# Value rows of the experts: summed by VectorE on the residual row instead of by TensorE in PSUM

## The chip, the cores and the metric

One core of one Trainium2 chip runs the whole step. The metric is the device time of one execution in microseconds (us). The kernel before took 2659.16 us (median of three runs, 2646.86 to 2667.52). The engines are called as in the profile: PE (TensorE matmul), PEld (its weight loads), DVE (VectorE), ACT (ScalarE), POOL (GpSimd), SP (SyncE). POOL issues the gathers, SP the loads of the weights.

## The reference, cut to what matters

One layer runs over 512 prompt rows and 32 sample rows of width 1024, in float32. It has two kinds of attention, output projections, and then a layer of experts (PEER): for each row, 8 heads pick 16 experts each out of 16384, so 128 experts a row. Of an expert, one row of `u` makes a score and one row of `v` is added, weighted:

```python
ue = jnp.take(u, eidx, axis=0)
act = jax.nn.gelu(jnp.einsum("nhkd,nd->nhk", ue, xb), approximate=False)
ve = jnp.take(v, eidx, axis=0)
return jnp.einsum("nhk,nhkd->nd", (g * act.astype(jnp.float32)).astype(ve.dtype), ve)
...
x = x + _peer(_rmsnorm(x, norm2_g), ...)
y = rmsnorm(x) * final_g
```

`xb` is the normed row, `g` the softmax over the 16 scores of a head. Every row needs its own 128 rows of `u` and `v`, so they are gathered from memory, 8 KB for a pair.

## The kernel before, in words

**Tiles.** The 544 rows are five tiles: four of 128 prompt rows (a row to a partition), and the 32 sample rows. A tile has a *front* (attention, projections, the choice of its experts) and its *slots*: slot j gathers the j-th expert of each of the 128 rows, a block of 128 x 2048 floats, 1 MB. A tile of prompt rows has 128 slots; the sample tile packs its 32 x 128 experts onto 128 partitions and has 32. In all there are 544 slots.

**A slot.** POOL waits until the ring slot is free and issues the gather (`gather`, L600) into one of six ring buffers (`RING = 6`). DVE takes the dot product of the `u` half with `xb` (`dot`, L1552, which the trace shows as a long instruction and a short read of the accumulator). ACT takes the gelu (L898). The `v` half is then added in one of two ways, as the table `ADDERS` says:
- PE: DVE writes a diagonal matrix gelu x weight (`weigh`, L1563; nine buffers, `DIAGS`), and PE multiplies it with the `v` half into the PSUM accumulator `acc` (`add_v`, L1217). A float32 matmul stands in the trace as several records.
- DVE: it makes the coefficient in a column (L1570) and adds coefficient x `v` onto `vsum` (`add_v`, L1577).

Four slots are a *block*, two a *half*. In the first 11 blocks of the kernel three of four slots go to DVE; in blocks 19 to 29 of each prompt tile all go to PE; else the last of four goes to DVE. PE opens `acc` with the residual row `x2` (`seed`, L1207), and adds `vsum` at the end (`close`, L1228). `finish` norms `acc` and stores the result.

**The order.** All engines walk one list, `PLAN`, each in its own program order. While the slots of tile t run, the front of tile t+1 is spread between its 64 halves (`spread`), in pieces: attention first (DVE takes a maximum of scores that PE has just made, L1411; ACT exponentiates; PE turns and multiplies), then the projections, whose weights SP loads in chunks of 1 MB through three buffers (`wbuf`; DVE works on their results at L1421 and L1432, ACT at L874), then the scores and the top-k search on DVE (L1438, L1443, L1449). On DVE a half is two dots and then two `weigh` or `add_v`, and the piece of the front comes behind it. PE runs the adds of a half after the pieces of that half. The sample tile's slots run last, in a loop, with no front beside them.

A ring slot is free for the next gather when its dot is taken and the engine that adds its value row is done with it.

## Time and profile before

| | |
|---|---|
| time, median of 3 runs | 2659.16 us (2646.86 to 2667.52) |
| span of the profiled execution, first to last instruction | 2671.0 us |
| PE busy | 2152.5 us, 81% of the span |
| DVE busy | 1434.8 us, 54% |
| ACT busy | 524.8 us, 20% |
| POOL busy | 671.1 us, 25% |
| data moved by DMA | 765.82 MB, of which the gathers' queue moved 570.46 MB |

The profiled execution is one more execution, not among the three; its span is 11.8 us above their median and 3.5 us above the highest. Busy time is time in which an engine has an instruction running; a busy PE is not a PE at its peak, since its matmuls overlap. The fronts and the slots load the engines differently, so the shares over the whole span are means over stages. The slots run from about 496 us to the end.

### The profile page before, as it was taken

To read this page: it belongs to the slowest core of one execution; us is meant where nothing else is said; L and a number is where in the kernel's file an instruction comes from. 1 tells how busy PE (TensorE), PEld (TensorE's weight loads), DVE (VectorE), ACT (ScalarE), POOL (GpSimd) and SP (SyncE) were. 2 spreads that over 40 slices of the span, in tenths; PEclk is the share of its full clock that TensorE was granted. 3 is DMA by queue.
4 is the path that set the end of the run, shared out by engine and by line. 5 is a ranking of instruction groups with operands and counts; after the bars stand their busy time and mean duration, and the time that the engine had idled before them with its cause. 6 is when DMAs were issued, how large, how long until landed. Compare 5 with 4: busy or idle time off the path is not lost. (4 is left out here: it accounts for less than half of the span.)

```text
span 2671.0 us, 23686 instructions
## 1 busy us (share of the span) xinstructions
PE 2152.5 (81%) x7804; PEld 1230.3 (46%) x7804; DVE 1434.8 (54%) x3480; ACT 524.8 (20%) x1354; POOL 671.1 (25%) x694
## 2 busy tenths in 40 slices
PE   7989889987698876897887778888765898987766
PEld 6845566455346632444562234456322344664211
DVE  0111105654554397666448865654795566337956
ACT  2321111110341101441110133301111332010111
POOL 0000000233222133233223422322333223223433
PEclk9988999999678987888998887999987787778788
DMA  9832455798769987678999866799989567888887
GB/s 275 272 91 86 136 185 173 290 361 316 266 231 333 331 322 298 257 272 325 367 376 334 346 243 247 299 378 334 396 308 387 221 248 285 304 310 310 313 329 314
DMA packets 271239, 765.82 MB, mean 287 GB/s; under 512 B 22736, under 2 KB 191744, under 8 KB 201488
## 3 DMA queue, kind: packets, MB, share of 16 engines
q0 software_dynamic: 78336, 570.46, 55.6%
q1 hardware_dynamic: 156848, 155.52, 18.6%
q10 hardware_dynamic: 35936, 38.35, 4.3%
q8 instruction: 62, 1.02, 0.2%
q14 instruction: 57, 0.47, 0.0%
HBM read 745.56 MB, written 18.30 MB: 286 GB/s over the span
## 5 line engine op out<-in xcount | busy, mean ns | idle before, releaser
L1217 PE MATMUL acc<-ring,diag 128*128 128x512 f32 (+1 forms) x1720 | 950.3, 705 | 272.2 <-DVE diag L1563 264.7
L600 POOL DMA_INDIRECT ring<-in_uv,stage x544 | 614.0, 1129 | 1471.1 <-PE acc L1217 877.0
L1552 DVE CUSTOM_DVE_ANT_0 ring<-ring,xb 128x1024 f32<-128x1024 f32 x544 | 651.5, 1221 | 209.1 <-DMA ring<-in_uv,stage 199.7
L1217 PEld LDWEIGHTS acc<-ring,diag 128*128 128x128 f32 (+1 forms) x1720 | 362.2, 222 | 783.4 <-issue 425.9
L898 ACT ACTIVATE gel<-dots 128x1 f32<-128x1 f32 x544 | 105.6, 201 | 1059.0 <-DVE dots L1552 1040.8
L1563 DVE TENSOR_SCALAR diag<-ident,gel,gw 128x128 f32<-128x128 f32 x406 | 141.8, 357 | 213.0 <-ACT gel L898 200.7
L1001 PE MATMUL pz<-F,wbuf 128*128 128x416 f32 (+1 forms) x656 | 244.8, 533 | 3.6 <-issue 1.4
L1001 PEld LDWEIGHTS pz<-F,wbuf 128*128 128x128 f32 (+1 forms) x656 | 127.1, 196 | 114.7 <-issue 114.7
L618 POOL COPY stage<-idx 128x4 int32<-128x4 int32 x130 | 50.9, 392 | 505.6 <-DVE gw L1511 486.6
L1411 DVE TENSOR_REDUCE nmax<-ps 128x1 f32<-128x128 f32 (+4 forms) x72 | 35.6, 495 | 236.9 <-PE ps L1058 81.5
L1577 DVE SCALAR_TENSOR_TENSOR vsum<-ring,coefd,vsum 128x1024 f32<-128x1024 f32 x109 | 140.3, 1287 | 4.0
L1183 PE MATMUL ps<-F,wbuf 128*128 128x128 f32 (+1 forms) x1024 | 132.3, 291 | 10.2 <-DMA wbuf<-in_peer_wq 5.9
L1183 PEld LDWEIGHTS ps<-F,wbuf 128*128 128x128 f32 x1024 | 130.1, 208 | 22.0 <-issue 13.5
L898 ACT ACT_TABLE_LOAD x65 | 83.4, 1283 | 26.2 <-issue 22.5
L1001 PE MATMUL pz<-wbuf,F 128*128 128x256 f32 (+1 forms) x384 | 85.7, 383 | 0.0
L1001 PE MATMUL pz<-ring,wbuf 128*128 128x128 f32 (+1 forms) x656 | 79.5, 280 | 6.7 <-PE pz L1001 2.8
L1001 PEld LDWEIGHTS pz<-ring,wbuf 128*128 128x128 f32 (+1 forms) x656 | 75.1, 190 | 13.9 <-issue 11.2
L1411 DVE TENSOR_REDUCE nmax<-pz 128x1 f32<-128x256 f32 (+3 forms) x48 | 28.6, 596 | 96.9 <-PE pz L1050 46.5
L1138 PEld LDWEIGHTS ps<-F,wbuf 128*128 128x128 f32 x512 | 69.1, 218 | 17.8 <-issue 6.5
L1001 PEld LDWEIGHTS pz<-wbuf,F 128*128 128x128 f32 (+1 forms) x384 | 65.8, 172 | 21.8 <-issue 5.4
L1138 PE MATMUL ps<-F,wbuf 128*128 128x128 f32 (+1 forms) x512 | 69.7, 300 | 6.9 <-ACT F L829 3.4
L1076 PE MATMUL pt<-ident,F 128*128 128x128 f32 (+2 forms) x224 | 34.3, 271 | 47.8 <-DVE F L1396 47.6
(259 smaller groups left out, 1954.4 us busy)
## 6 DMA issues: line engine op xcount, KB each, us to landing
wbuf<-in_w_in SPq DMA_DIRECT2D x52, 1024.0 KB
wbuf<-in_peer_wq SPq DMA_DIRECT2D x40, 1024.0 KB
wbuf<-in_w_pa SPq DMA_DIRECT2D x20, 1024.0 KB
wbuf<-in_w_o SPq DMA_DIRECT2D x20, 1024.0 KB
wbuf<-in_w_pb SPq DMA_DIRECT2D x20, 512.0 KB
ring<-in_uv,stage POOLq DMA_INDIRECT x544
zT<-F ACTq DMA_DIRECT2D x28, 208.0 KB, 2.9
qT<-zT ACTq DMA_DIRECT2D x4, 768.0 KB, 6.8
```

The lines of the kernel that those rows point to most:

```text
L600: pool.indirect_dma_start(out=ring[:, slot, :], out_offset=None, in_=d["uv"], in_offset=bass.IndirectOffsetOnAxis(ap=stage[:, a, k:k + 1], ...
L618: nc.gpsimd.tensor_copy(stage[:, a, :], idx[:, t % 2, BLOCK * b:BLOCK * b + BLOCK]).then_inc(staged[a], 1)
L898: nc.scalar.activation(gel[:, slot:slot + 1], dots[:, slot:slot + 1], ACT.Gelu).then_inc(gelued, 1)
L1001: last = nc.tensor.matmul(out, left, right, start=(k == 0), stop=(k == KT - 1))
L1076: last = nc.tensor.transpose(pt[0:w, j * nq:(j + 1) * nq], p[0:nq, j * P:j * P + w], ident[0:nq, 0:nq])
L1138: last = nc.tensor.matmul(ps[f % 2][:, 0:nq], wa[:, k, j * P:(j + 1) * P], fa(t).oaT[:, k, 0:nq], start=(k == 0), stop=(k == 7))
L1183: last = nc.tensor.matmul(ps[f % 2][:, 0:nq], w[:, k, j * P:(j + 1) * P], fa(t).xbT[:, k, 0:nq], start=(k == 0), stop=(k == 7))
L1217: last = nc.tensor.matmul(acc[0:nq, c * 512:(c + 1) * 512], diag[:, parity, 0:nq], ring[:, slot, D + c * 512:D + (c + 1) * 512], start=Fal ...
L1411: nc.vector.tensor_reduce(nmax[0:nq, n:n + 1], score_bank(t, n)[0:nq, 0:nk], AX.X, ALU.max, negate=True).then_inc(maxed, 1)
L1552: nc.vector.tensor_tensor_reduce(out=u, in0=u, in1=xb[:, t % 2, :], scale=1.0, scalar=0.0, op0=ALU.mult, op1=ALU.add, accum_out=dots[:, sl ...
L1563: nc.vector.tensor_scalar(diag[:, parity, 0:nq], pick[:, 0:nq], gel[:, slot:slot + 1], g, ALU.mult, ALU.mult).then_inc(coef_set, 1)
L1577: last = nc.vector.scalar_tensor_tensor(vsum[:, :], v, c, vsum[:, :], ALU.mult, ALU.add)
```

## The change

- `ADDERS`, `vsum`, `diag`, `coefd` and the accumulator `acc` are gone. DVE adds every value row (`add_v`): coefficient x `v` onto `xsum`, a pair of buffers of which a tile uses one, and in which the front has put the residual row. PE takes no part in the slots, but for two matmuls at the end of the kernel that fold the sample tile's four groups of partitions (`fold`).
- ACT makes the coefficient: behind each gelu it multiplies by the expert's weight into a column `cf` (`weigh`).
- A gather waits for DVE's add alone. DVE's add waits for ACT's coefficient and for the add before it.
- The attention of tile t+1 no longer waits for PE's `seed`: `xsum` has two buffers, and its operand `foxq` lies in the one that tile t-1 used, so it waits for that tile's result.
- The sample tile's slots are written out, not looped.

```diff
-DIAGS = 9
-EARLY = 11
-LATE = (19, 30)
...
-    return plan + [("experts_loop", TILES - 1, 0), ("finish", TILES - 1, 0)]
+    plan += [("experts", TILES - 1, b) for b in range(SLOTS // 4 // HALF)]
+    return plan + [("finish", TILES - 1, 0)]
...
-    counts, out = {"tensor": 0, "vector": 0}, []
-    for s in range(SLOTS * (TILES - 1) + SLOTS // 4):
-        who_early = "vector" if s < BLOCK * EARLY and s % BLOCK else None
-        late = s < SLOTS * (TILES - 1) and LATE[0] <= s % SLOTS // BLOCK < LATE[1]
-        who = "vector" if s % BLOCK == BLOCK - 1 and not late else "tensor"
-        who = who_early or who
-        counts[who] += 1
-        out.append((who, counts[who]))
...
-        vsum = sb("vsum", [P, D])
-        coefd = sb("coefd", [P, STAGES])
+        xsum = sb("xsum", [P, 2, D])
+        cf = sb("cf", [P, RING])
...
+        def y_sum(t):
+
+            return ps_all[0:DEC, :] if t == TILES - 1 else xsum[:, t % 2, :]
+
+        def foxq(t):
+
+            return xsum[0:16, t % 2, :].rearrange("p (h q) -> p h q", h=HEADS)
...
                     if s >= RING:
-                        who, count = ADDERS[s - RING]
-                        waits = [(dotted, s - RING + 1), (adders[who], count)]
+                        waits = [(v_added, s - RING + 1)]
                     gather(k, a, s % RING, waits)
...
-            def gelu(slot, count):
-                act.wait_ge(dotted, count)
+            def gelu(s):
+
+                slot = s % RING
+                act.wait_ge(dotted, s + 1)
                 nc.scalar.activation(gel[:, slot:slot + 1], dots[:, slot:slot + 1], ACT.Gelu).then_inc(gelued, 1)
 
+            def weigh(t, s, j):
+
+                slot = s % RING
+                act.wait_ge(gelued, s + 1)
+                nc.scalar.activation(cf[:, slot:slot + 1], gel[:, slot:slot + 1], ACT.Copy, scale=gw[:, t % 2, j:j + 1]
+                                     ).then_inc(weighed, 1)
+
             def experts(t, b, h):
-                s0 = SLOTS * t + BLOCK * b + HALF * h
-                for s in range(s0, s0 + HALF):
-                    gelu(s % RING, s + 1)
-
...
+                j0 = BLOCK * b + HALF * h
+                if j0 == 0:
+                    act.wait_ge(route_ready, t + 1)
+                    if t == TILES - 1:
+                        act.wait_ge(packed, 16 * 9)
+                for j in range(j0, j0 + HALF):
+                    gelu(SLOTS * t + j)
+                    weigh(t, SLOTS * t + j, j)
...
             def finish(t):
                 nq = rows_of(t)
-                act.wait_ge(summed, t + 1)
-                act.wait_ge(dotted, SLOTS * t + slots_of(t))
-                rms_sum(xb[0:nq, t % 2, :], acc[0:nq, :], nq, 8)
+                act.wait_ge(v_added, SLOTS * t + slots_of(t))
+                if t == TILES - 1:
+                    act.wait_ge(summed, 1)
+                rms_sum(xb[0:nq, t % 2, :], y_sum(t), nq, 8)
                 rms_root_(nq, 8, 9)
                 act.wait_ge(y_ready, t + 1)
...
-            def add_v(t, slot, parity, count):
-
-                nq = rows_of(t)
-                pe.wait_ge(coef_set, count)
-                for c in range(2):
-                    last = nc.tensor.matmul(acc[0:nq, c * 512:(c + 1) * 512], diag[:, parity, 0:nq],
-                                            ring[:, slot, D + c * 512:D + (c + 1) * 512],
-                                            start=False, stop=False, skip_group_check=True)
-                last.then_inc(v_added, 1)
-
...
-            def close(t):
-
-                nq = rows_of(t)
-                pick = ident if t < TILES - 1 else sel32
-                pe.wait_ge(v_added_dve, v_adds("vector", SLOTS * t + slots_of(t)))
-                for c in range(2):
-                    last = nc.tensor.matmul(acc[0:nq, c * 512:(c + 1) * 512], pick[:, 0:nq],
-                                            vsum[:, c * 512:(c + 1) * 512], start=False, stop=True,
-                                            skip_group_check=True)
...
+            def fold(t):
...
+                pe.wait_ge(v_added, SLOTS * t + slots_of(t))
                 for c in range(2):
...
+                    last = nc.tensor.matmul(ps[c][0:nq, :], sel32[:, 0:nq], xsum[:, t % 2, c * 512:(c + 1) * 512],
+                                            start=True, stop=True)
                 last.then_inc(summed, 1)
...
-            held = None
             for what, t, p in PLAN:
-                if what in ("experts", "experts_loop") and held:
-                    experts(*held)
-                    held = None
-                if what == "experts":
-                    if p == 0:
-                        seed(t)
-                    held = (t, p // 2, p % 2)
-                elif what == "experts_loop":
-                    seed(t)
-                    experts_loop(t)
-                elif what in pe_stages:
+                if what in pe_stages:
                     pe_stages[what](t, p)
+            fold(TILES - 1)
...
-                if t:
-                    dve.wait_ge(seeded, t)
+                if t >= 2:
+                    dve.wait_ge(y_ready, t - 1)
+                if t == TILES - 1:
+                    nc.vector.memset(xsum[DEC:2 * DEC, t % 2, :], 0.0).then_inc(rest_cleared, 1)
+                    nc.vector.memset(xsum[2 * DEC:P, t % 2, :], 0.0).then_inc(rest_cleared, 1)
...
-            def weigh(t, slot, parity, g, gelus, adds):
-
-                nq = rows_of(t)
-                if adds is not None:
-                    dve.wait_ge(v_added, adds)
-                dve.wait_ge(gelued, gelus)
-                pick = ident if t < TILES - 1 else sel32
-                nc.vector.tensor_scalar(diag[:, parity, 0:nq], pick[:, 0:nq], gel[:, slot:slot + 1], g,
-                                        ALU.mult, ALU.mult).then_inc(coef_set, 1)
...
-            def add_v(slot, turn, g, gelus, coefs, adds):
-
-                dve.wait_ge(gelued, gelus)
-                c = coefd[:, turn:turn + 1]
-                nc.vector.tensor_scalar(c, gel[:, slot:slot + 1], g, None, ALU.mult).then_inc(coefd_set, 1)
-                dve.wait_ge(coefd_set, coefs)
-                v = ring[:, slot, D:2 * D]
-                if adds is None:
-                    last = nc.vector.tensor_scalar(vsum[:, :], v, c, None, ALU.mult)
-                else:
-                    dve.wait_ge(v_added_dve, adds)
-                    last = nc.vector.scalar_tensor_tensor(vsum[:, :], v, c, vsum[:, :], ALU.mult, ALU.add)
-                last.then_inc(v_added_dve, 1)
...
+            def add_v(t, s):
+
+                slot = s % RING
+                dve.wait_ge(weighed, s + 1)
+                dve.wait_ge(v_added, s)
+                total = xsum[:, t % 2, :]
+                nc.vector.scalar_tensor_tensor(total, ring[:, slot, D:2 * D], cf[:, slot:slot + 1], total,
+                                               ALU.mult, ALU.add).then_inc(v_added, 1)
...
             def experts(t, b, h):
-                if b == 0 and h == 0:
+                j0 = BLOCK * b + HALF * h
+                if j0 == 0:
...
+                        dve.wait_ge(rest_cleared, 2)
+                half = range(SLOTS * t + j0, SLOTS * t + j0 + HALF)
+                for s in half:
+                    dot(t, s)
+                for s in half:
+                    add_v(t, s)
...
-                dve.wait_ge(summed, t + 1)
-                nc.vector.scalar_tensor_tensor(xb[0:nq, t % 2, :], acc[0:nq, :], sstat[0:nq, 8:9], gfrow[0:nq, :],
+                nc.vector.scalar_tensor_tensor(xb[0:nq, t % 2, :], y_sum(t), sstat[0:nq, 8:9], gfrow[0:nq, :],
                                                ALU.mult, ALU.mult).then_inc(y_ready, 1)
```

What moves. On DVE, in the top-k search of the third tile, which lies beside the second tile's slots (blocks 19 and 20 of that tile; `MAX` is the search, the two `ISA` rows are a dot and the read of its sum), before:

```order
L1563 TENSOR_SCALAR diag<-ident,gel,gw 128x128 x2
L1438 MAX F<-F 128x8 x16
L1552 ISA ring,dots<-ring,xb 128x1024
L1552 ISA dots 128x1
L1552 ISA ring,dots<-ring,xb 128x1024
L1552 ISA dots 128x1
L1563 TENSOR_SCALAR diag<-ident,gel,gw 128x128 x2
```

and of the change:

```order
L1335 MAX F<-F 128x8 x16
L1450 ISA ring,dots<-ring,xb 128x1024
L1450 ISA dots 128x1
L1450 ISA ring,dots<-ring,xb 128x1024
L1450 ISA dots 128x1
L1460 SCALAR_TENSOR_TENSOR xsum<-ring,cf,xsum 128x1024 x2
```

Two diagonals of 128 columns have become two adds of 1024 columns; the number of dots and the search stand as they were.

On DVE, in the attention of the third tile beside the second tile's slots (`nmax` is the maximum that waits for PE's scores), before:

```order
L1411 TENSOR_REDUCE nmax<-pz 128x1 x2
L1552 ISA ring,dots<-ring,xb 128x1024
L1552 ISA dots 128x1
L1552 ISA ring,dots<-ring,xb 128x1024
L1552 ISA dots 128x1
L1563 TENSOR_SCALAR diag<-ident,gel,gw 128x128
L1570 TENSOR_SCALAR coefd<-gel,gw 128x1
L1577 SCALAR_TENSOR_TENSOR vsum<-ring,coefd,vsum 128x1024
```

and of the change:

```order
L1308 TENSOR_REDUCE nmax<-pz 128x1 x2
L1450 ISA ring,dots<-ring,xb 128x1024
L1450 ISA dots 128x1
L1450 ISA ring,dots<-ring,xb 128x1024
L1450 ISA dots 128x1
L1460 SCALAR_TENSOR_TENSOR xsum<-ring,cf,xsum 128x1024 x2
```

A half that had one diagonal, one coefficient and one add has two adds; the maxima keep their place ahead of the next half.

On PE, from the last projection of the second tile's front to the attention of the third tile's (`kaT` x `qT`), before:

```order
L1183 MATMUL ps<-F,wbuf 128x128 x48
L1217 MATMUL acc<-ring,diag 128x512 x4
L1183 MATMUL ps<-F,wbuf 128x128 x32
L1195 MATMUL ps<-wbuf,F 128x128 x16
L1217 MATMUL acc<-ring,diag 128x512 x68
L1228 MATMUL acc<-vsum,ident 128x512 x2
L1207 MATMUL acc<-x2,ident 128x512 x2
L1217 MATMUL acc<-ring,diag 128x512 x4
L1036 MATMUL ps<-kaT,qT 128x384
L1050 MATMUL ps<-bias,ident 128x256
```

and of the change:

```order
L1121 MATMUL pt<-ident,xb 128x128 x4
L1121 MATMUL po<-ident,xb 128x128 x4
L1134 MATMUL ps<-F,wbuf 128x128 x128
L1146 MATMUL ps<-wbuf,F 128x128 x16
L987 MATMUL ps<-kaT,qT 128x384
L1001 MATMUL ps<-bias,ident 128x256
```

The matmuls of the projection follow each other with none of the slots' between them, and the next tile's attention follows them at once in PE's program.

## Rows read from the trace of the kernel before

**Rows 1.** The page: busy us of each engine; ACT's gelus (busy, mean ns, idle before).

```profile
PE 2152.5 (81%) x7804; PEld 1230.3 (46%) x7804; DVE 1434.8 (54%) x3480; ACT 524.8 (20%) x1354; POOL 671.1 (25%) x694
...
L898 ACT ACTIVATE gel<-dots 128x1 f32<-128x1 f32 x544 | 105.6, 201 | 1059.0 <-DVE dots L1552 1040.8
```

**Rows 2.** Stages (windows): length, busy PE, PEld, DVE, ACT, POOL; granted clock; DMA share, GB/s.

```profile
495.90:641.00 145.10, 131.26 (x477) 83.98 (x476) 92.62 (x150) 16.62 (x68) 51.66 (x48) 0.96 0.94 357
698.70:805.30 106.60, 94.16 (x273) 48.00 (x272) 62.83 (x149) 53.20 (x109) 24.72 (x30) 0.80 0.63 228
805.30:943.70 138.40, 122.20 (x655) 90.82 (x654) 55.09 (x134) 20.11 (x57) 26.01 (x29) 0.93 0.94 330
943.70:1031.00 87.30, 56.22 (x93) 21.88 (x92) 84.65 (x266) 7.74 (x27) 28.74 (x30) 0.80 0.76 288
...
1055.50:1209.50 154.00, 130.46 (x361) 63.13 (x361) 98.46 (x208) 65.95 (x132) 42.49 (x49) 0.83 0.74 279
1209.50:1388.30 178.80, 145.00 (x702) 101.99 (x703) 89.61 (x192) 23.40 (x74) 48.34 (x50) 0.90 0.97 351
1388.30:1512.50 124.20, 89.21 (x160) 35.98 (x159) 108.75 (x315) 10.98 (x43) 52.75 (x50) 0.84 0.89 337
...
2219.30:2411.30 192.00, 168.57 (x680) 112.46 (x679) 83.58 (x181) 20.71 (x76) 47.62 (x47) 0.73 0.85 300
2411.30:2540.50 129.20, 97.80 (x202) 41.00 (x201) 111.50 (x332) 13.11 (x47) 52.06 (x51) 0.84 0.84 318
...
2575.60:2671.00 95.40, 56.88 (x101) 11.69 (x100) 59.07 (x111) 9.08 (x36) 39.00 (x34) 0.80 0.85 344
```

**Rows 3.** Who waited for whom, whole span: us in total, times, longest us.

```profile
POOL ring L600 <- PE acc L1217: 877.0, 154, 22.0
DVE diag L1563 <- ACT gel L898: 201.7, 52, 13.6
DVE ring L1552 <- DMA ring<-in_uv,stage: 199.7, 139, 6.2
```

**Rows 4.** Timeline of DVE in attention: start, us, instruction, idle before it and its releaser.

```profile
1128.12 0.56 DVE L1411 TENSOR_REDUCE nmax<-pz 128x1 f32<-128x384 f32 x1 [1.84 <-PE pz L1050]
1129.59 0.56 DVE L1411 TENSOR_REDUCE nmax<-pz 128x1 f32<-128x384 f32 x1 [0.91 <-PE pz L1050]
1130.06 1.22 DVE L1552 CUSTOM_DVE_ANT_0 ring<-ring,xb 128x1024 f32<-128x1024 f32 x1
...
1132.97 1.28 DVE L1577 SCALAR_TENSOR_TENSOR vsum<-ring,coefd,vsum 128x1024 f32<-128x1024 f32 x1
1134.18 1.22 DVE L1552 CUSTOM_DVE_ANT_0 ring<-ring,xb 128x1024 f32<-128x1024 f32 x1
...
1137.15 0.16 DVE L1391 RECIPROCAL rinv<-rsum 128x2 f32<-128x2 f32 x1
```

**Rows 5.** Timeline of DVE in the top-k search.

```profile
1447.96 1.22 DVE L1552 CUSTOM_DVE_ANT_0 ring<-ring,xb 128x1024 f32<-128x1024 f32 x1
...
1450.26 0.77 DVE L1563 TENSOR_SCALAR diag<-ident,gel,gw 128x128 f32<-128x128 f32 x2
1450.94 1.22 DVE L1552 CUSTOM_DVE_ANT_0 ring<-ring,xb 128x1024 f32<-128x1024 f32 x1
```

**Rows 6.** Groups by line, 1055.5 to 1209.5 us: busy, mean ns, idle before, releasers.

```profile
L1411 DVE TENSOR_REDUCE nmax<-ps 128x1 f32<-128x384 f32 x12 | 6.7, 558 | 29.2 <-PE ps L1050 17.9 <-PE ps L1058 10.7 <-issue 0.5
L1411 DVE TENSOR_REDUCE nmax<-pz 128x1 f32<-128x384 f32 x12 | 6.7, 558 | 21.4 <-PE pz L1050 14.2 <-PE pz L1058 7.2
```

**Rows 7.** Granted clock beside two such pieces (windows, columns as in rows 2).

```profile
1126.00:1130.00 4.00, 3.93 (x17) 2.30 (x18) 1.25 (x4) 2.44 (x4) 1.19 (x2) 1.00 0.76 252
1614.00:1619.00 5.00, 5.00 (x12) 2.67 (x12) 1.33 (x3) 1.71 (x3) 0.00 (x0) 0.50 0.79 315
```

**Rows 8.** Timeline of DVE in the second of them.

```profile
1615.21 0.69 DVE L1411 TENSOR_REDUCE nmax<-pz 128x1 f32<-128x512 f32 x1 [2.66 <-PE pz L1050]
1618.36 0.69 DVE L1411 TENSOR_REDUCE nmax<-pz 128x1 f32<-128x512 f32 x1 [2.46 <-PE pz L1050]
```

132 lines of the change are left out of this document (12 added, 120 removed).

## The prediction, made before the result

> **What bounds the kernel now.** The page says that PE is the busiest engine, 81% against DVE's 54% [rows 1]. That invites the thought that taking work off PE must help. The means hide stages with different limits, so I read the stages next, then who waited for whom, then DVE's own timeline.
>
> Cut by what the next tile's front does, the slots of one tile fall into three long stages [rows 2]. POOL's count tells how many slots a stage holds: a block of four slots is four gathers and one copy, so x50 is ten blocks and x30 six.
> - Attention (1055.5 to 1209.5 us): ten blocks in 154.0 us. DVE is busy 98.5 us and DMA only 0.74. What fills DVE's gaps are the maxima, which wait 50.6 us for PE's scores [rows 6]. The timeline [rows 4] shows how: DVE waits 1.84 and 0.91 us in a piece, and then works through the slots without a pause: 1130.06 to 1137.15 is one block, and the next piece begins at once. DVE is never short of a gathered row there. DVE and its round trip to PE set the pace.
> - Projections (1209.5 to 1388.3 us): DMA share 0.97 at 351 GB/s. The weights share the DMA engines with the gathers, and DMA sets the pace. The same stage beside the first and the fourth tile's slots has DMA 0.94 and 0.85, with PE busy 122.2 of 138.4 us and 168.6 of 192.0 us: there PE has a part in it.
> - Top-k search (1388.3 to 1512.5 us): DVE is busy 108.8 of 124.2 us, and beside the first tile's slots 84.7 of 87.3 us. DVE is the bound.
>
> POOL waits 877.0 us for PE's adds [rows 3]. That number is large and mostly harmless: a gather that goes out later costs only where DVE then finds its row missing, and that wait is 199.7 us in the whole kernel.
>
> **The change, part by part.**
>
> *DVE per block.* Two dots take 2.30 us (1447.96 to 1450.26 in rows 5). An add of 1024 columns takes 1.28 us, and what follows it starts after 1.21 us (1132.97 to 1134.18 in rows 4). Of the two adds of a half, the second waits for the first one's end, so I put 2.52 us for the pair. A half is 4.82 us, a block 9.64 us. Before, a block with one add by DVE took 7.09 us [rows 4], and one with none 2 x 2.98 = 5.96 us [rows 5]. So a block gains 2.55 us in attention and 3.68 us in the top-k search.
>
> *Attention.* The four prompt tiles have 6 + 10 + 10 + 10 = 36 such blocks (the first tile has fewer, since projections precede them). 36 x 2.55 = **+92 us**. Nothing hides it, as DVE works through its slots without a pause.
>
> *Top-k search.* Again 36 blocks: 36 x 3.68 = 132 us. DVE is idle 2.6, 15.5 and 17.7 us in three of the four stages [rows 2], and I take 15 for the fourth, together some 50 us. Those waits are for gathered rows, at the start of the stage, while the extra work is spread over it. I let 27 us of them take it up: **+105 us** (ends 82 and 132).
>
> *Waits for PE in attention.* This is where PE's relief can show. Twelve pieces wait 50.6 us, 4.2 us each, so some 202 us in four fronts. With PE at 2.4 GHz (granted clock 1.00 [rows 7]) a piece waits 2.75 us [rows 4]; at 1.2 GHz (granted clock 0.50 [rows 7]) 2.66 + 2.46 = 5.12 us [rows 8]. Without the slots' matmuls ahead of them the scores are never late, but PE also has less to do, and the granted clock can fall more often. All 48 pieces fast would be 132 us, -70; all slow 246 us, +44. I take **0**, between the two, and keep both ends.
> The Trainium skill (TensorE: Matmul & The Clock Gate, "What's actually happening") says that the throttled state is the default and activity releases it, so it speaks against taking matmuls away. By it alone the end of +44 would hold. The trace shows both levels in this phase, so I don't go all the way.
>
> *Projections.* The first and the fourth tile's slots moved 330 GB/s x 138.4 us and 300 GB/s x 192.0 us; at the 351 GB/s of the second tile's they would take 130 and 164 us: -8 and -28. In the two stages that are already at 0.97, DVE has 89 us idle for an extra 25.5 us each, and I put +3 each for the part that lands behind a wait in DVE's program order. Together **-30 us**. Ends: -46, if the 0.97 goes to 1 as well (two times 5 us) and nothing is paid; +15, if the two stages pay all of their 25.5 us.
>
> *The start of the first tile's slots* (495.9 to 641.0 us): three of four adds are DVE's already, DMA share 0.94. **-8 us** (ends -9 and 0).
>
> *The sample tile* (2575.6 to 2671.0 us): eight blocks x 9.64 = 77 us of DVE in 95.4 us. DMA share is 0.85, and the gathers need no longer go round by PE. **-5 us** (ends -14 and 0).
>
> *ACT.* One more instruction a slot, which I put at the gelu's 0.20 us [rows 1]: 109 us for an engine that is 20% busy. The first coefficient is made while DVE takes the second dot (1.15 us). Where ACT comes late from the exponentials of a piece, the add waits 0.2 us more; behind the add stand the next dots, the next piece of the front, and by it PE. 48 such halves give 10 us at most; **+6 us** (ends 0 and 25, if all 272 halves pay 0.1 us).
>
> *What else moves.* POOL waits for DVE's add alone; its order is the same. `seed` and `close` go, ten pairs of matmuls, which the 0 above includes. The wait of the attention for the last tile's result is over when `finish` is, and that stands ahead of it on DVE already: nothing. SP's weights wait for PE as before.
>
> *Sum:* 92 + 105 + 0 - 30 - 8 - 5 + 6 = +160 us. The profiled execution's span was 2671.0 us, so 2831 us, and as it lies 11.8 us above the median of the runs, **2819 us** for the median, 6% above 2659.
>
> **The rivals.**
> - *Cold PE.* All pieces wait as in rows 8 (+44) and the projections, whose matmuls then run at 1.2 GHz more often, give nothing back (+30): 2893 us. For it: the granted clock of every stage is below 1, down to 0.73, so that parts of each ran at the lower level, with PE busy for most of the time [rows 2]. Against: in the projections PE works in long bursts, and there the granted clock is 0.93 and 0.90 beside the first two tiles' slots, if only 0.73 beside the fourth's [rows 2]. This is the skill's rule above, as a mechanism of this kernel.
> - *Nothing absorbed.* DVE's waits in program order are not filled: the top-k search pays 132, not 105, and the projections +15, not -30: +72, 2891 us. For it: DVE cannot work on slots while its next instruction waits for a projection. Against: in those stages it waits for gathered rows too, and that wait takes extra work for free.
> - *Fast PE.* All pieces at 2.75 us (-70), the projections at -46, the top-k search at 82: 2659 + 160 - 70 - 16 - 23 = 2710 us.
> - *PE was the bound after all (faster).* The extra DVE work is some 92 + 132 + 92 in the projections' 36 blocks + 20 in the sample tile, 336 us. If DVE's waits for gelus (201.7 us), which are delayed by PE in ACT's program order, and for gathered rows (199.7 us) both go [rows 3], that is 401 us back, and 2659 + 336 - 401 = 2594 us. It decides from 336 us of relief on. For it: 81% against 54% and POOL's 877 us. Against: neither wait is long in the attention and the top-k stages, where two thirds of the extra work lies, and DMA at 0.97 does not let the waits of the projections go.
> - *A draw.* The relief is about the extra work, 2660 us: it needs both ends of the projections and of the waits for PE, and an idle DVE in the top-k stages that I don't see.
>
> **How the numbers follow.** Forecast 0.55, own range 2765 to 2875 us. Cold PE 0.12, nothing absorbed 0.08, fast PE 0.10, faster 0.07, a draw 0.08. The first four are slower by more than 1% (about what a measurement can tell here): 0.85; within 1% 0.08; faster 0.07. The range from 2715 to 2910 us leaves out the faster case, the draw and the outer part of fast PE below, and a few per cent above.
>
> **What would show it.** In the profile after: DVE busy about 1434.8 + 544 - 109 adds more at 1.28 us (557) less 430 diagonals at 0.385 (0.77 for two [rows 5]; 166), so about 1825 us, and near 97% in the top-k stage, which takes 150 us instead of 124; the attention stage 180 us instead of 154; a piece's waits between 2.75 and 5.1 us; the projections of the second tile within 6 us of 178.8; POOL waiting for DVE's adds where it waited for PE. The forecast is wrong if the attention stage stays near 154 us or if DVE waits long for gelus or rows in the top-k stage.

## The result, and the profile after

The changed kernel takes **2951.4 us** (median of 4 runs, 2948.0 to 2958.2) where the kernel before takes 2662.0 us (median of 4): a ratio of 1.112 (95% interval 1.108 to 1.117). I had forecast slower, 2819 us with a range from 2715 to 2910 us. The sign was right, the size was not: the profiled spans differ by 2946.8 - 2671.0 = 275.8 us, and I had 160.

The page of the kernel after: busy time, granted clock in 40 slices, and the groups of the experts (busy, mean ns | idle before, releaser).

```profile
PE 1412.8 (48%) x6048; PEld 990.1 (34%) x6048; DVE 1811.2 (61%) x3368; ACT 678.4 (23%) x1898; POOL 829.2 (28%) x694
...
PEclk9988999985568555556765555577655555555555
...
L576 POOL DMA_INDIRECT ring<-in_uv,stage x544 | 771.6, 1418 | 1586.5 <-DVE xsum L1460 1456.6
...
L1460 DVE SCALAR_TENSOR_TENSOR xsum<-ring,cf,xsum 128x1024 f32<-128x1024 f32 x544 | 697.9, 1283 | 256.8 <-ACT cf L855 228.4
L1450 DVE CUSTOM_DVE_ANT_0 ring<-ring,xb 128x1024 f32<-128x1024 f32 x544 | 645.3, 1220 | 25.8 <-DMA ring<-in_uv,stage 23.9
...
L855 ACT ACTIVATE cf<-gel,gw 128x1 f32<-128x1 f32 x544 | 160.2, 295 | 17.7
```

PE fell from 81% [rows 1] to 48%, DVE rose to 61%, and no engine is now busy for two thirds of the span. DVE's busy time, 1811.2 us, is where the forecast had it (1825). The second line is the news. From the tenth slice on, the granted clock is mostly 5, which is PE's lower level, 1.2 GHz, throughout a slice. A gathered row is hardly ever late any more: 23.9 us, where DVE waited 199.7 [rows 3].

Who waited for whom, columns as in [rows 3]:

```profile
POOL ring L576 <- DVE xsum L1460: 1456.6, 222, 23.2
DVE xsum L1460 <- ACT cf L855: 228.4, 89, 20.5
```

POOL now waits for DVE as it waited for PE. DVE's wait for ACT has not gone with PE's work: 201.7 us for the gelu became 228.4 us for the coefficient.

The stages after, in windows with the columns of [rows 2]. They are cut at the same slots as before: the first 40 slots, then attention, projections and top-k search beside the first tile's slots, the same and the plain rest beside the second's, projections and top-k search beside the fourth's, and the sample tile.

```profile
498.10:633.30 135.20, 116.90 (x440) 79.42 (x439) 96.76 (x120) 29.93 (x109) 61.04 (x51) 0.94 0.98 384
691.40:831.40 140.00, 79.81 (x200) 45.82 (x200) 79.08 (x144) 58.77 (x133) 29.28 (x30) 0.50 0.47 172
831.40:974.20 142.80, 87.90 (x564) 80.31 (x564) 76.60 (x134) 27.07 (x81) 35.48 (x30) 0.80 0.92 324
974.20:1083.40 109.20, 0.00 (x0) 0.00 (x0) 107.08 (x267) 14.81 (x51) 33.03 (x29) 0.50 0.61 222
1102.90:1316.70 213.80, 104.64 (x241) 54.91 (x241) 125.19 (x200) 76.08 (x172) 57.57 (x51) 0.51 0.55 210
1316.70:1500.90 184.20, 100.05 (x579) 91.49 (x579) 115.34 (x184) 34.95 (x114) 63.34 (x52) 0.73 0.96 347
1500.90:1649.10 148.20, 0.00 (x0) 0.00 (x0) 145.26 (x314) 22.77 (x83) 63.76 (x49) 0.50 0.72 276
1649.10:1668.60 19.50, 0.00 (x0) 0.00 (x0) 19.08 (x25) 3.98 (x16) 14.19 (x11) 0.50 0.99 377
2482.50:2667.80 185.30, 126.17 (x582) 112.48 (x581) 110.36 (x171) 32.66 (x117) 62.59 (x49) 0.55 0.86 311
2667.80:2821.20 153.40, 3.55 (x20) 2.73 (x18) 148.18 (x331) 24.31 (x86) 68.38 (x50) 0.51 0.70 267
2853.60:2946.80 93.20, 3.62 (x4) 0.54 (x4) 80.03 (x103) 19.79 (x69) 35.55 (x34) 0.50 0.84 350
```

Summed over the four prompt tiles, from both traces ("start" is the first 48 slots):

| stage | before | after | change | forecast |
|---|---|---|---|---|
| before the first slot | 495.9 | 498.1 | +2 | 0 |
| start of the first tile's slots | 202.9 | 193.3 | -10 | -8 |
| attention | 620.0 | 813.6 | **+194** | +92 and 0 for waits |
| projections | 684.7 | 698.6 | **+14** | -30 |
| top-k search | 462.3 | 559.1 | +97 | +105 |
| plain rest of a tile | 109.9 | 90.9 | -19 | none |
| sample tile | 95.3 | 93.2 | -2 | -5 |

(ACT's +6 stood in no one stage.) So the top-k search, both ends of the program and DVE's own work were foreseen. The miss lies in the attention, about 100 us, and in the projections, 44 us.

In the second tile's attention stage the window says how the loss splits. It is 213.8 - 154.0 = 59.8 us longer. DVE is busy 125.19 - 98.46 = 26.7 us longer, against the 10 x 2.55 that I had. Most of the rest is in two groups, the maxima that wait for PE's scores:

```profile
L1308 DVE TENSOR_REDUCE nmax<-ps 128x1 f32<-128x384 f32 x12 | 6.7, 557 | 46.6 <-PE ps L1001 31.6 <-PE ps L1009 14.9
L1308 DVE TENSOR_REDUCE nmax<-pz 128x1 f32<-128x384 f32 x12 | 6.7, 556 | 34.3 <-PE pz L1001 22.8 <-PE pz L1009 11.5
```

80.9 us where it was 50.6 [rows 6], +30.3 us. Over the 48 pieces the sum in the traces went from 230.6 to 320.4 us, +90. (The forecast had started from 202, the second tile's mean times 48.) DVE's timeline beside such a piece (columns as in [rows 4]):

```profile
1206.19 0.56 DVE L1308 TENSOR_REDUCE nmax<-pz 128x1 f32<-128x384 f32 x1 [3.46 <-PE pz L1001]
1208.92 0.56 DVE L1308 TENSOR_REDUCE nmax<-pz 128x1 f32<-128x384 f32 x1 [2.17 <-PE pz L1001]
1209.40 1.21 DVE L1450 CUSTOM_DVE_ANT_0 ring<-ring,xb 128x1024 f32<-128x1024 f32 x1
...
1212.06 2.67 DVE L1460 SCALAR_TENSOR_TENSOR xsum<-ring,cf,xsum 128x1024 f32<-128x1024 f32 x2 [0.30 <-ACT cf L855]
1214.65 1.22 DVE L1450 CUSTOM_DVE_ANT_0 ring<-ring,xb 128x1024 f32<-128x1024 f32 x1
...
1216.94 2.67 DVE L1460 SCALAR_TENSOR_TENSOR xsum<-ring,cf,xsum 128x1024 f32<-128x1024 f32 x2
1219.53 0.16 DVE L1288 RECIPROCAL rinv<-rsum 128x2 f32<-128x2 f32 x1
```

The piece waits 3.46 + 2.17 = 5.63 us; the same piece of before waited 2.75 [rows 4]. The block behind it runs from 1209.40 to 1219.53, 10.13 us with a wait of 0.30 for ACT, so 9.83 of work against the 9.64 that I had summed. The granted clock is 0.50 in this piece and in each of the 48; before, it was 1.00 throughout in 22 of them.

The first piece of a tile is a case of its own. Its queries `qT` are loaded by ACT's queue, and the load now lands late:

```profile
1111.32 0.38 ACTq L791 DMA_DIRECT2D qT<-zT  x1
...
1127.14 1.61 PE L987 MATMUL ps<-kaT,qT 64*128 64x384 f32 x2 [159.87 <-DMA qT<-zT]
...
1129.95 0.56 DVE L1308 TENSOR_REDUCE nmax<-ps 128x1 f32<-128x384 f32 x1 [12.57 <-PE ps L1001]
```

These rows say that DVE stands idle for 12.57 us because PE began at 1127.14, 15.8 us after the load was issued. The first pieces of the four fronts wait 60.0 us together, where it was 42.8. So of the +90 us, 17 are theirs and 73 belong to the 44 ordinary pieces (187.8 to 260.4 us).

### The profile page after: what moved, and what is told of

Same layout as the page of the kernel before. It is cut to its first block, busy times and chain, and to the rows that moved or that the text cites. A ratio compares the mean times of both kernels' runs of the same rounds, so it can differ in the third digit from the quotient of the medians.

```text
span 2946.8 us, 20298 instructions
## 1 busy us (share of the span) xinstructions
PE 1412.8 (48%) x6048; PEld 990.1 (34%) x6048; DVE 1811.2 (61%) x3368; ACT 678.4 (23%) x1898; POOL 829.2 (28%) x694
## 4 chain that ended last, share of the span: by engine, by line
PE 38%; DVE 33%; DMA 12%; issue 8%; ACT 7%; ACTq 1%; SPq 0%; DVEq 0%; POOL 0%; PEldq 0%; POOLq 0%
DVE xsum L1460 16%; PE pz L952 13%; DVE ring L1450 6%; PE ps L1134 5%; PE ps L987 3%; PE ps L1089 3%; PE pz L987 2%; ACT L849 2%; DMA wbuf<-in_peer_wq 2%; DVE F L1340 2%; DMA wbuf<-in_w_o 2%; DMA wbuf<-in_w_pa 2%; DMA qT<-zT 2%; DMA wbuf<-in_w_in 2%; PE ps L1111 2%
## 5 line engine op out<-in xcount | busy, mean ns | idle before, releaser
L576 POOL DMA_INDIRECT ring<-in_uv,stage x544 | 771.6, 1418 | 1586.5 <-DVE xsum L1460 1456.6
L1460 DVE SCALAR_TENSOR_TENSOR xsum<-ring,cf,xsum 128x1024 f32<-128x1024 f32 x544 | 697.9, 1283 | 256.8 <-ACT cf L855 228.4
L1450 DVE CUSTOM_DVE_ANT_0 ring<-ring,xb 128x1024 f32<-128x1024 f32 x544 | 645.3, 1220 | 25.8 <-DMA ring<-in_uv,stage 23.9
L987 PE MATMUL ps<-kaT,qT 64*128 64x128 f32 (+4 forms) x96 | 64.2, 766 | 622.8 <-DMA qT<-zT 401.4
L987 PEld LDWEIGHTS ps<-kaT,qT 64*128 64x128 f32 (+1 forms) x96 | 19.3, 254 | 638.3 <-issue 636.6
L1134 PE MATMUL ps<-F,wbuf 128*128 128x128 f32 (+1 forms) x1024 | 161.7, 328 | 43.1 <-DMA wbuf<-in_peer_wq 33.5
L1134 PEld LDWEIGHTS ps<-F,wbuf 128*128 128x128 f32 x1024 | 156.7, 246 | 48.7 <-DMA wbuf<-in_peer_wq 34.4
L1027 PE MATMUL pt<-ident,F 128*128 128x128 f32 (+2 forms) x224 | 52.9, 377 | 240.4 <-DVE F L1293 240.4
L855 ACT ACTIVATE cf<-gel,gw 128x1 f32<-128x1 f32 x544 | 160.2, 295 | 17.7
L1027 PEld LDWEIGHTS pt<-ident,F 128*128 128x128 f32 (+2 forms) x224 | 36.2, 221 | 253.2 <-DVE F L1293 252.0
L1089 PE MATMUL ps<-F,wbuf 128*128 128x128 f32 (+1 forms) x512 | 94.5, 365 | 55.5 <-DMA wbuf<-in_w_pa 27.1
L1089 PEld LDWEIGHTS ps<-F,wbuf 128*128 128x128 f32 x512 | 91.9, 282 | 58.8 <-DMA wbuf<-in_w_pa 28.1
```

Source lines behind the costliest of these rows:

```text
L576: pool.indirect_dma_start(out=ring[:, slot, :], out_offset=None, in_=d["uv"], in_offset=bass.IndirectOffsetOnAxis(ap=stage[:, a, k:k + 1], ...
L855: nc.scalar.activation(cf[:, slot:slot + 1], gel[:, slot:slot + 1], ACT.Copy, scale=gw[:, t % 2, j:j + 1]).then_inc(weighed, 1)
L987: nc.tensor.matmul(s[0:nq, 0:bank], q, kk[:, 0:bank], start=True, stop=False)
L1027: last = nc.tensor.transpose(pt[0:w, j * nq:(j + 1) * nq], p[0:nq, j * P:j * P + w], ident[0:nq, 0:nq])
L1089: last = nc.tensor.matmul(ps[f % 2][:, 0:nq], wa[:, k, j * P:(j + 1) * P], fa(t).oaT[:, k, 0:nq], start=(k == 0), stop=(k == 7))
L1134: last = nc.tensor.matmul(ps[f % 2][:, 0:nq], w[:, k, j * P:(j + 1) * P], fa(t).xbT[:, k, 0:nq], start=(k == 0), stop=(k == 7))
```

## The experiments

Theory 1, formed on these rows: PE, left with little to do, runs at 1.2 GHz, and each piece's scores come later to a DVE that waits for them. The rivals: DVE's longer work alone makes the loss (the adds, or the coefficients from ACT), or the order of the instructions on DVE does.

A ratio is against the kernel before, measured again beside the run (medians 2653.0 to 2664.9 us). The changed kernel was not, so differences from its 2951.4 us carry a few us of that spread. Stages are read from the profiled execution.

### e1: the changed kernel, PE kept busy through all slots

```diff
+        spare = psum("spare", 512)
...
+            def beat(t, b, h):
+                for k in range(HALF * h, HALF * h + HALF):
+                    pe.wait_ge(dotted, SLOTS * t + BLOCK * b + k + 1)
+                    for c in range(2):
+                        nc.tensor.matmul(spare[:, 0:512], ident[:, :], gfrow[:, 0:512], start=True, stop=True)
...
+                if what == "experts":
+                    if held is None:
+                        pe.wait_ge(rows_landed, 32)
+                    else:
+                        beat(*held)
+                    held = (t, p // 2, p % 2)
```

> The changed kernel, with two matmuls of 128x512 per slot given back to PE, behind the slot's dot, from constants into a spare bank: no result of theirs is used and nobody waits for them. Theory 1 (the clock): the changed kernel is slow beyond DVE's extra work because PE, left with little to do, runs at the lower clock, and DVE waits for its scores. Then the granted clock comes back to 0.8 or more, a piece of attention waits some 4.2 us where it waited 6.7, and the time falls by 48 x 2.5 = 120 us less what the new matmuls cost in PE's order: about 2850 us (2810 to 2890). Theory 2 (DVE's work and the order alone): the clock does not matter, the time stays within 15 us of 2951 or rises.

Measured: 2961.6 us, ratio 1.117 (1.109 to 1.125), mean clock 0.861. Theory 1's 2850 us missed, and the total is what theory 2 said, although the clock came back as theory 1 wanted. The stages say more (their execution took 2942.5 us, the fastest of five): attention 813.6 to 746.2 us, but the start of the first tile's slots 193.3 to 239.5 and the projections 698.6 to 714.0. The second tile's attention stage, and PE's groups from 500 to 700 us of this run:

```profile
1134.90:1332.10 197.20, 153.69 (x394) 74.19 (x393) 125.33 (x200) 76.57 (x172) 57.59 (x51) 0.78 0.60 229
```

```profile
L1167 PE MATMUL spare<-gfrow,ident 128*128 128x512 f32 x170 | 75.5, 597 | 3.1 <-DVE dots L1465 1.7
L953 PE MATMUL pz<-wbuf,F 128*128 128x256 f32 x288 | 63.1, 379 | 0.0
```

At a clock of 0.78 instead of 0.51 the stage is 16.6 us shorter with the same work on DVE. At the start PE is full with projections, and the spare matmuls take 75.5 us of its time. Two effects of opposite sign, so the next job separates them (e5).

### e2: the changed kernel, half of each value row added

```diff
-                total = xsum[:, t % 2, :]
-                nc.vector.scalar_tensor_tensor(total, ring[:, slot, D:2 * D], cf[:, slot:slot + 1], total,
+                total = xsum[:, t % 2, 0:512]
+                nc.vector.scalar_tensor_tensor(total, ring[:, slot, D:D + 512], cf[:, slot:slot + 1], total,
```

> The changed kernel, where DVE adds only 512 of the 1024 columns of every value row (the other half of the sum is left out): an add takes some 0.53 us less, 544 of them 290 us. Theory 1 and 2 alike have DVE as the bound in attention and the top-k search, 72 blocks of four slots: 153 us less at least; if the projections pay DVE's work too, all 144 us more of theirs and the rest: 2951 - 153 = 2798 us if they don't, down to 2680 us if they do. A rival by which the clock alone sets the time: less than 60 us faster.

Measured: 2804.9 us, ratio 1.056 (1.049 to 1.064). Top-k search 559.1 to 485.0 us, -74, and attention -60; projections only -5.5. The second tile's top-k stage:

```profile
1460.00:1587.50 127.50, 0.00 (x0) 0.00 (x0) 124.30 (x316) 22.77 (x83) 57.40 (x48) 0.50 0.82 312
```

DVE is busy 124.30 of 127.50 us, before the edit 145.26 of 148.20: 21.0 us less work, 20.7 us less time. Between these two the top-k stage is DVE's work and nothing else. The projections, on the other hand, hardly follow DVE. The total is near the 2798 us expected if they don't.

### e3: the kernel before, PE's matmuls of the slots on 64 columns instead of 512

```diff
-                    last = nc.tensor.matmul(acc[0:nq, c * 512:(c + 1) * 512], diag[:, parity, 0:nq],
-                                            ring[:, slot, D + c * 512:D + (c + 1) * 512],
+                    last = nc.tensor.matmul(acc[0:nq, c * 512:c * 512 + 64], diag[:, parity, 0:nq],
+                                            ring[:, slot, D + c * 512:D + c * 512 + 64],
```

> The kernel before, where PE's adds take 64 of every 512 columns (the rest of the sum is left out); DVE, ACT, POOL and the DMAs do all that they did. Theory 1: the granted clock falls to 0.65 or so, a piece's wait rises from 4.7 to 5.6 us or more (48 of them: +45 to +95 us), while waits for gelus and for free ring slots fall; the time goes up, to about 2700 us, though PE has less to do. Theory 2: less work on PE can only help: 2600 to 2660 us.

Measured: 2718.3 us, ratio 1.025 (1.017 to 1.032). Work was only taken away, and the kernel is slower by 53 us (the kernel before had 2664.9 us beside it). Its mean clock is 0.671 where before had 0.861. The second tile's attention stage and its maxima:

```profile
1056.00:1233.60 177.60, 128.83 (x361) 78.29 (x361) 98.41 (x208) 65.73 (x132) 45.72 (x47) 0.54 0.65 237
```

```profile
L1411 DVE TENSOR_REDUCE nmax<-ps 128x1 f32<-128x384 f32 x12 | 6.7, 558 | 39.0 <-PE ps L1050 22.4 <-PE ps L1058 16.6
L1411 DVE TENSOR_REDUCE nmax<-pz 128x1 f32<-128x384 f32 x12 | 6.7, 558 | 35.0 <-PE pz L1050 22.8 <-PE pz L1058 12.3
```

This is the cleanest run of all. DVE is busy 98.41 us, as before (98.46). The clock fell from 0.83 to 0.54, the maxima wait 74.0 us instead of 50.6 (+23.4), and the stage is 177.6 - 154.0 = 23.6 us longer. It holds in the kernel before, with none of the change's other edits. All four attention stages together lose 82 us, and the 48 waits grow by 84 (230.6 to 314.8), all of it in the ordinary pieces (the first ones take 43.3 us against 42.8). The projections gain 14 us, the top-k search 17 and the first slots 8. The time was expected at about 2700 us.

### e4 and e8: the changed kernel, the work of a piece parted on DVE

A piece on DVE is two things: it merges and stores what the last piece made (which frees buffers for PE and ACT), and takes the maxima of the new scores. In the change both stand behind the half's adds. e4 puts the first part between the dots and the adds, e8 ahead of the dots (`between()` above the first loop). The maxima stay behind the adds.

```diff
+            def experts(t, b, h, between=None):
...
                 for s in half:
                     dot(t, s)
+                if between:
+                    between()
                 for s in half:
                     add_v(t, s)
...
+                    if then == "front" and ATTEND <= q < NORM_O:
+                        experts(t, p // 2, p % 2, lambda: attend_a(i, q - ATTEND))
+                        attend_b(i, q - ATTEND)
...
```

> The changed kernel with DVE's program order altered: the first part of an attention piece (the merge that PE waits for, and the stores) stands between the two dots and the two adds of the half before it, the maxima stay behind the adds. If DVE's waits for PE's scores are on the path, 2.5 us of each is now covered by the adds: 48 x 2.5 = 120 us less, 2830 us. If something else sets the pace there (the gathers, ACT), the time stays within 20 us of 2951.

> The changed kernel with the first part of an attention piece ahead of the half's dots, so that dots and adds (4.8 us) cover PE's round trip, where e4 covered it by the adds alone (2825 us, DVE's waits for scores 212 us). If the exponentials that the merge needs are ready by then: 48 x 2.3 us less again, 2825 - 90 = 2735 us. If ACT is not done with them, DVE waits for ACT in place of PE: 2790 to 2830 us.

Measured: e4 2824.9 us, ratio 1.064 (1.057 to 1.072); e8 2777.0 us, ratio 1.044 (1.040 to 1.049). The clock stays low (0.656 in both). Attention falls from 813.6 to 688.6 and to 639.6 us, and the waits for scores from 320 to 212 and to 142 us; nothing else moves by more than 7 us. e4 is where it was expected (2830 us); e8 lies between its two cases (2735, or 2790 to 2830), and DVE's wait for ACT's coefficients is no longer there than in the changed kernel (216.0 us against 228.4). So a late score costs most where nothing stands between the merge and the maxima. The slower clock does its harm through that open round trip: it is a wait of the order as much as of the clock.

### e5: the changed kernel, PE kept busy beside the attention alone

As e1, with `beat` called for halves 22 to 35 of the first tile and 0 to 21 of the others:

```diff
-                        beat(*held)
+                        n = 2 * held[1] + held[2]
+                        if 22 <= n < 36 if held[0] == 0 else n < 22:
+                            beat(*held)
```

> As e1 (matmuls that nobody waits for), but only beside the pieces of attention, so that the projections of the first tile's start are left alone. In e1 the attention stages fell from 814 to 746 us in all, and that start and the projections grew by 62 us. Theory 1 (the clock slows the attention): attention 746 us again, the rest as in the changed kernel, 2951 - 67 = 2884 us (2870 to 2900). Theory 2 (what e1 gained and lost were one thing, work moved from one stage to the other): about 2950 us.

Measured: 2886.1 us, ratio 1.087 (1.081 to 1.092), 65 us below the changed kernel. The second tile's attention stage and its maxima:

```profile
1080.90:1279.00 198.10, 157.24 (x393) 76.36 (x393) 125.27 (x199) 75.96 (x171) 57.67 (x51) 0.77 0.60 225
```

```profile
L1325 DVE TENSOR_REDUCE nmax<-ps 128x1 f32<-128x384 f32 x12 | 6.7, 558 | 41.2 <-PE ps L1002 28.6 <-PE ps L1010 12.7
L1325 DVE TENSOR_REDUCE nmax<-pz 128x1 f32<-128x384 f32 x12 | 6.7, 556 | 23.8 <-PE pz L1002 15.9 <-PE pz L1010 7.9
```

Matmuls whose results nobody reads were added, DVE has the same work (125.27 us against 125.19), and the stage is 15.7 us shorter, for 15.9 us less of waiting (80.9 to 65.0). With e3 this shows theory 1 from both sides. Over all 48 pieces the waits fall from 320 to 265 us and the attention stages by 55 us. That is 55 of the 73 us of the ordinary pieces; the first pieces stay at 60.0 us, so their 17 are not the clock's. Why the ordinary ones do not come back in full is not shown: the clock is 0.77 and not 0.83, and the spare matmuls stand in PE's queue ahead of the scores.

### e6: the changed kernel, DVE makes the coefficient

```diff
+                dve.wait_ge(gelued, s + 1)
+                nc.vector.tensor_scalar(cf[:, slot:slot + 1], gel[:, slot:slot + 1], gw[:, t % 2, j:j + 1], None, ALU.mult
+                                        ).then_inc(weighed, 1)
```

and ACT's `weigh` is not called.

> The changed kernel with the coefficient made by DVE (a multiply of one column ahead of each add, 0.20 us and its wait) instead of by ACT behind the gelu. In the DVE-bound stages, 288 slots, DVE works 0.2 us and more longer for each: +70 us. If ACT's coefficients are what DVE waits for (228 us of waits in the changed kernel), part of it comes back: 30 us in attention and projections. Theory (those waits are ACT standing behind PE's projections, not the coefficient's own time): 3010 to 3040 us. Rival (the coefficient's way over ACT is the cost): 2950 us or less.

Measured: 2989.8 us, ratio 1.123 (1.117 to 1.129), 38 us above the changed kernel, between the two cases: 20 us under the theory's 3010, 40 above the rival's 2950. The top-k search has some 22 us of it (559.1 to 580.8 us). DVE's column takes 208 ns and makes 113 us of DVE work, and DVE's wait for ACT goes from 228.4 to 192.1 us. So most of that wait is ACT standing behind other work, and some 36 us are the coefficient's way over ACT. Handing the coefficient to ACT saves time all the same, although ACT takes 295 ns for it.

### e7: the kernel before, with the order of e8

The parted piece of e8, in `half_block` of the kernel before; PE and DVE share the value rows as they did.

```diff
-            def half_block(t, q, h, j, more, first):
+            def half_block(t, q, h, j, more, first, between=None):
...
+                if between:
+                    between()
                 for k in range(HALF * h, HALF * h + HALF):
```

> The kernel before, with the first part of an attention piece (the merge that PE waits for, and the stores) ahead of the half's dots instead of behind its adds; the maxima stay where they were. DVE's dots and diagonals (3.0 to 4.1 us) then cover PE's round trip (2.75 to 5.1 us). If DVE sets the pace in attention also in the kernel before, as I read it: 44 pieces x 2.5 us = 110 us less, 2555 us; PE is busy for 85% there and may not follow: then 30 to 60 us less, 2600 to 2635 us. If PE or the gathers were the bound: 2650 us or more.

Measured: **2566.2 us**, ratio 0.965 (0.960 to 0.969): 88 us or 3.5% faster than the kernel before, which had 2654.6 us beside it, and the lowest time of all that was run. It lies between the 2555 us and the 2600 to 2635 us expected. Clock 0.887. Its second attention stage, its maxima there, and a piece on DVE's timeline:

```profile
1040.50:1169.50 129.00, 113.40 (x358) 54.97 (x359) 97.21 (x208) 63.85 (x131) 50.87 (x48) 0.95 0.89 331
```

```profile
L1414 DVE TENSOR_REDUCE nmax<-ps 128x1 f32<-128x384 f32 x12 | 6.5, 554 | 8.2 <-PE ps L1058 5.7 <-PE ps L1050 2.5
L1414 DVE TENSOR_REDUCE nmax<-pz 128x1 f32<-128x384 f32 x12 | 6.4, 553 | 7.5 <-PE pz L1058 7.3
```

```profile
1060.61 0.62 DVE L1396 SCALAR_TENSOR_TENSOR F<-F,coef 128x384 f32<-128x384 f32 x1
1061.14 1.22 DVE L1559 CUSTOM_DVE_ANT_0 ring<-ring,xb 128x1024 f32<-128x1024 f32 x1
...
1063.43 0.77 DVE L1570 TENSOR_SCALAR diag<-ident,gel,gw 128x128 f32<-128x128 f32 x2
1064.12 1.25 DVE L1414 TENSOR_REDUCE nmax<-pz 128x1 f32<-128x384 f32 x2
```

The merge ends, two dots and two diagonals follow, and the maxima find their scores ready. They wait 15.7 us instead of 50.6, and the stage is 25 us shorter. The clock rose too, 0.83 to 0.95 in this stage, and this run doesn't part the two gains; e8, whose clock stayed at 0.656, shows that the order alone takes most of the waits away.

### e9 and e10: the kernel before, fewer adds on DVE

The opposite of the change: all four slots of a block go to PE from block 1 of each prompt tile on, not from block 19 (the first 11 blocks of the kernel stay as they are). e9 is that alone, e10 has the order of e7 as well.

```diff
-LATE = (19, 30)
+LATE = (1, 30)
```

> The kernel before with one number changed: blocks 1 to 29 of a prompt tile give all their adds to PE, where blocks 1 to 18 gave the last of four to DVE (the first tile's start stays as it was). DVE saves 1.1 us a block (7.09 against 5.96) in 36 blocks of attention, PE gains 1.3 us at 2.4 GHz or more at 1.2. If DVE alone is the bound in attention: 2662 - 40 = 2620 us. If PE (busy 85% there) is about as close: within 20 us of 2662, or slower.

> e7 (2566 us) with the number of e9. With the round trip to PE covered, DVE's own work is what is left in attention: 2566 - 40 = 2525 us, if PE keeps up. If PE is the next bound, at 87% busy in e7's attention, it is slower than e7: 2570 to 2600 us.

Measured: e9 2598.4 us, ratio 0.980 (0.974 to 0.987), clock 0.908; e10 2569.6 us, 0.968 (0.962 to 0.975), clock 0.909. With more work for PE and less for DVE the kernel is 2% faster, 22 us below the 2620 expected: attention 620.0 to 568.3 us, projections 684.7 to 665.1. DVE loses 62 adds, and its busy time in attention falls by 37 us; the waits for scores fall by only 11 (230.6 to 219.7), though the clock rose from 0.83 to 0.93 in the second tile's attention. So most of this gain is DVE's own work, and not e3 turned round.

With e7's order nothing is left to gain by it: 2569.6 us cannot be told from e7's 2566.2, and the 2525 us missed. Its waits for scores are 160 us where e7 has 100, which fits the other case, PE as the next bound.

### e11: e8 and e5 together

The kernel of e8, with e5's spare matmuls added:

```diff
+                        n = 2 * held[1] + held[2]
+                        if 22 <= n < 36 if held[0] == 0 else n < 22:
+                            beat(*held)
```

> e8 (the changed kernel with the merge ahead of the dots, 2777 us) with e5's idle matmuls beside attention. Alone, those gave 65 us by the clock. If the clock costs only by DVE's wait for scores, which e8 has cut from 320 to 142 us, less of it is left to gain: 25 to 45 us, 2735 to 2750 us. If the clock costs by another way also (ACT's or DVE's waits behind PE): 65 us again, 2710 us.

Measured: 2739.2 us, ratio 1.030 (1.023 to 1.038), 38 us below e8, as expected; waits for scores 142 to 105 us. The clock still pays with the better order, but less than with the old one (38 against 65 us), as it should if the order covers part of the same wait. No version in which DVE adds all rows in full came below the kernel before.

### e12: the changed kernel, one eighth of each value row added

```diff
-                total = xsum[:, t % 2, :]
-                nc.vector.scalar_tensor_tensor(total, ring[:, slot, D:2 * D], cf[:, slot:slot + 1], total,
+                total = xsum[:, t % 2, 0:128]
+                nc.vector.scalar_tensor_tensor(total, ring[:, slot, D:D + 128], cf[:, slot:slot + 1], total,
```

> The changed kernel where DVE adds 128 of the 1024 columns of every value row (seven eighths of the sum are left out). Against e2 (512 columns, 2805 us) an add is shorter by another 0.4 us. In the DVE-bound attention and top-k stages, 288 slots: 115 us less. The question is the projections: they took 699 us in the changed kernel, 693 with half adds, and 670 in e3, where DVE only wrote diagonals and PE was as cold. If DVE's work there hides wholly, they stay at 690 and the time is 2690 us. If it is what separates the changed kernel from e3, they fall to 670 us: 2665 us.

Measured: 2707.7 us, ratio 1.019 (1.014 to 1.023), above both cases (2690 and 2665). Here DVE has less work than in the kernel before (1312.7 us against 1434.8), and PE has no part in the slots. So it is about what the relief of PE would be worth, in the order of the changed kernel, with an add at the price of the diagonal that it replaces (356 and 357 ns). The second attention stage and its adds:

```profile
1056.80:1241.10 184.30, 104.29 (x241) 54.83 (x241) 88.38 (x199) 76.19 (x172) 44.64 (x51) 0.50 0.65 249
```

```profile
L1460 DVE SCALAR_TENSOR_TENSOR xsum<-ring,cf,xsum 128x128 f32<-128x128 f32 x40 | 14.2, 356 | 7.7 <-ACT cf L855 6.4
```

DVE is busy 10 us less than in [rows 2] (98.46) and the stage is 30 us longer. Attention as a whole is 708.8 us, 89 above before; the projections are 679.7, 5 below. In this order, taking PE out of the slots is a loss before DVE has any more to do.

## Why the prediction was right, and where it was wrong

**What bounds the kernel: right.** DVE and its round trip to PE set the pace in the attention, DVE in the top-k search. The busy shares of [rows 1] did mislead: the engine at 81% was not the one to relieve.

**DVE per block, top-k search: right.** +97 us against +105. DVE's work in the four stages grew by 132 us, as summed, and 35 of them went into idle time, where I had let 27. The second tile's stage takes 148.2 us for the 150 forecast. DVE is busy 98% of it.

**DVE's adds in the attention: right.** 26.7 us in ten blocks, 98 in the 36, against +92.

**Waits for PE in the attention: the step that failed.** The text reads "I take **0**, between the two, and keep both ends", -70 and +44; measured is +90. Two things were wrong with it. First, the choice. I had the clock's two levels side by side [rows 7] and the two waits that belong to them (2.75 and 5.12 us), and took it that PE would go on mixing them. The matmuls that I removed were what kept the clock up: read at each of the 48 pieces, the granted clock is 0.50 after the change, where 22 of them stood wholly at 2.4 GHz before (1.00). e3 shows the effect alone (+23.4 us of waits in ten blocks, with nothing added), e5 undoes 55 us of the 73. Second, the end was too small. My 246 us for all pieces at 1.2 GHz came from one piece; there are 320 us. That piece did not run at 1.2 GHz throughout. I had cut its window [rows 7] short; over the whole of it, from the merge's end on, the clock is 0.61:

```profile
1612.60:1619.10 6.50, 6.50 (x17) 3.25 (x16) 1.43 (x3) 2.67 (x5) 0.00 (x0) 0.61 0.80 318
```

It also has maxima of 512 columns [rows 8], where the fast one had 384 [rows 4], so the two rows differed in more than the clock. At 0.50 throughout, the same two pieces take 6.56 and 5.63 us. Most ordinary pieces take 4.4 to 7.1 us now, by the tile, and one in each tile 7.0 to 11.4. The first piece of each tile takes 18.8, 14.7, 15.2 and 11.2 us, 60 us together where it was 43; in the second and the third `qT` lands late. I had no term for that, and why it does is open. The rule that I had cited from the Trainium skill (TensorE: Matmul & The Clock Gate, "What's actually happening"), that the lower clock is the default and activity lifts it, spoke for the upper end, and the measurement sides with it: I should have given that rival more than 0.12.

**Projections: also failed, by less.** "-30 us", measured +14. What I read was that the first tile's stage is held up by PE. In e3, with light PE and DVE as before, it does take 131.1 us, where I had 130. But in the change it takes 142.8, and with an eighth of the adds (e12) still 139.4: the adds' length is only 3.4 of the 11.7 us between. In the second tile's stage I took 0.97 and 351 GB/s for DMA's limit at 178.8 us [rows 2]; e3 does it in 168.2 us at 368 GB/s. The change takes 184.2 us at 347 GB/s, and e12 the same 184 with 37 us less DVE work, so the adds' length is not what it pays for there. Only the fourth's gained, 192.0 to 185.3, of the 28 us I had for it, and e12's 173.5 shows that 12 us more of it are DVE's adds. The granted clock in the second's stage is 0.73 in the change, 0.74 in e12 and 0.77 in e3, so it hardly parts them.

Two things that I hadn't seen stand in the rows of the second tile's projections. The first is in the groups of DVE and of ACT:

```profile
L1460 DVE SCALAR_TENSOR_TENSOR xsum<-ring,cf,xsum 128x1024 f32<-128x1024 f32 x40 | 51.3, 1283 | 40.8 <-ACT cf L855 38.7
```

```profile
L823 ACT ACTIVATE F<-ps 128x128 f32<-128x128 f32 x16 | 4.4, 276 | 37.8 <-PE ps L1134 37.8
```

ACT waits 37.8 us for projections that PE is making, and the coefficients stand behind those instructions in ACT's order; DVE's adds wait 38.7 us for them, and the ring slots with the adds. So PE still holds up the slots, by way of ACT. The second is what PE waits for there (us in total, times, longest us):

```profile
PE ps L1134 <- DMA wbuf<-in_peer_wq: 14.2, 2, 10.9
PE ps L1089 <- DMA wbuf<-in_w_pa: 10.8, 2, 8.6
```

All waits of PE for weights are 33 us in this stage, where they were 10 before (20 in e3, 47 in e12), while DVE's waits for gathered rows went from 30.7 us to nothing. Read together: the gathers now run ahead, the weights come late on busy DMA engines, and PE, ACT and the adds wait in turn. That is a reading; no run tests it, and what part each wait has in the missing gain is open.

**Plain rest of a tile: missed.** No term stood for these two blocks, worth -19 us. Before, they took 25 us each (35 in the last tile); now they take 19.5 us, DVE busy 19.08: 2 x 9.64 us of DVE's work. The second tile's window of before says that DVE was not the limit there, but DMA:

```profile
1512.50:1537.70 25.20, 17.74 (x36) 6.83 (x34) 14.92 (x26) 1.62 (x8) 13.17 (x13) 0.93 0.99 399
```

e3, with light PE, still takes 26.1 us, so it was not PE's hold on the gathers either. The cause of this gain is not shown.

**Start of the slots, sample tile: right** (-10 for -8, -2 for -5).

**ACT: small, as forecast, with a price that was too low.** The coefficient takes 295 ns, not 200. In the second tile's attention stage it explains at most the idle time outside the maxima, 7.7 us where it was 4.9.

**The rivals.** "Cold PE" had the mechanism, and a time of 2893 us that was 58 us short: its +44 for the waits was +90, and its 0 for the projections +14. "PE was the bound after all" and "fast PE" are out: e12 shows what the relief buys with cheap adds, and it is negative. "Nothing absorbed" hit the projections' number (+15) by luck: it had the second and the third tile's stages pay for all of DVE's extra work, and with an eighth of the adds (e12) they are only 0.1 and 3.6 us shorter than in the change. Its top-k search, 132, was wrong.
